# The second feed-forward unit as eight products, and fewer, wider operations on the hidden activations

## The reference, cut to what matters

```python
def swiglu(hn, w_gate, w_up, w_down):
    return (jax.nn.silu(hn @ w_gate) * (hn @ w_up)) @ w_down
```

## Time and profile before

| what | us |
|---|---|
| median of 3 runs | 965.77 (965.2 to 968.26) |
| the profiled execution's own time | 965.3 |
| its span, first to last instruction | 963.2 |
| PE busy | 903.3 (94%) |
| VectorE busy | 662.5 (69%) |
| ScalarE busy | 452.3 (47%) |
| GpSimd busy | 234.3 (24%) |
| feed-forward units, first to last matmul | 582.5 to 949.5 |

### The profile page before, as it was taken

The page is one execution under the profiler, slowest core; times in us unless marked ns, Lnnn a source line. Parts: engine busy times, 40 slices in busy tenths (PEclk is TensorE's granted clock), DMA queues, the critical chain, the costliest instruction groups (busy, mean ns, idle before and its releaser), DMA issues.

```text
span 963.2 us, 17847 instructions
## 1 busy us (share of the span) xinstructions
PE 903.3 (94%) x7198; PEld 829.3 (86%) x7198; DVE 662.5 (69%) x1272; ACT 452.3 (47%) x831; POOL 234.3 (24%) x163
## 2 busy tenths in 40 slices
PE   5999999889999999999989998899999998999997
PEld 4999998756799889975569898899999998999996
DVE  4799974565445796121553678998869999779765
ACT  5553125566454473135425545455445555345442
POOL 3000001103000033300020022444544444545540
PEclk9999999899999999999999989799999999999999
DMA  8222206422442359268052003222242222222232
GB/s 231 91 86 89 89 2 230 161 71 88 138 131 76 103 182 329 100 233 335 9 168 66 24 1 137 88 89 88 90 127 91 88 88 89 88 88 88 99 126 93
DMA packets 81554, 110.55 MB, mean 115 GB/s; under 512 B 9505, under 2 KB 64674, under 8 KB 81090
## 3 DMA queue, kind: packets, MB, share of 16 engines
q1 hardware_dynamic: 81248, 109.37, 34.0%
q10 hardware_dynamic: 226, 0.05, 0.0%
HBM read 100.48 MB, written 8.93 MB: 114 GB/s over the span
## 4 chain that ended last, share of the span: by engine, by line
PE 70%; DVE 19%; issue 5%; ACT 4%; DMA 1%; SPq 1%; DVEq 0%; POOL 0%; ACTq 0%
PE pall L2303 20%; PE pall L2879 17%; PE pall L2315 6%; PE pall L2657 5%; PE pall L2888 4%; PE pall L2340 4%; DVE ring_lo L1412 2%; DVE pall L1409 2%; DVE g_part L1412 2%; PE pall L2708 2%; PE pall L2373 1%; DVE g_part_f L1406 1%; PE pall L2727 1%; PE pall L2327 1%; PE pall L2533 1%
## 5 line engine op out<-in xcount | busy, mean ns | idle before, releaser
L817 POOL TENSOR_TENSOR ring_lo<-w_raw,ring_hi 128x512 fp32r<-128x512 f32 (+1 forms) x128 | 174.2, 1374 | 266.0 <-ACT ring_hi L1271 265.2
L2879 PE MATMUL pall<-x_hi,ring_hi 128*128 128x272 f32 x304 | 91.2, 300 | 13.8 <-DVE gate_odd L1409 5.7
L2879 PE MATMUL pall<-x_sum,ring_hi 128*128 128x272 f32 x456 | 89.1, 291 | 4.3 <-ACT sq L1299 4.3
L2879 PE MATMUL pall<-x_lo,ring_hi 128*128 128x272 f32 x304 | 90.2, 297 | 0.0
L2879 PE MATMUL pall<-x_hi,ring_lo 128*128 128x272 f32 x304 | 90.1, 296 | 0.0
L1271 ACT ACTIVATE ring_hi<-w_raw 128x512 fp32r<-128x512 f32 (+1 forms) x128 | 75.4, 612 | 26.5 <-PE pall L2879 17.2
L2879 PE MATMUL pall<-g_part,ring_hi 128*128 128x272 f32 x448 | 84.5, 288 | 1.9 <-DVE z_down L1409 1.9
L2879 PEld LDWEIGHTS pall<-x_sum,ring_hi 128*128 128x128 f32 x456 | 73.0, 191 | 4.5 <-ACT sq L1299 4.5
L2303 PE MATMUL pall<-x_hi,w_hi 128*128 128x272 f32 x352 | 73.6, 290 | 0.5 <-issue 0.5
L2879 PEld LDWEIGHTS pall<-x_hi,ring_hi 128*128 128x128 f32 x304 | 59.8, 197 | 15.5 <-DVE gate_odd L1409 6.4
L2303 PE MATMUL pall<-x_hi,w_lo 128*128 128x272 f32 x352 | 72.9, 288 | 0.0
(11 more groups left out here) (464 smaller groups left out, 2393.8 us busy)
## 6 DMA issues: line engine op xcount, KB each, us to landing
w_raw<-in_w_gate SPq DMA_DIRECT2D x10, 1024.0 KB, 5.3
w_raw<-in_w_up SPq DMA_DIRECT2D x10, 1024.0 KB, 5.3
w_raw<-in_w_in SPq DMA_DIRECT2D x8, 1024.0 KB, 5.7
w_raw<-in_w_down SPq DMA_DIRECT2D x8, 1024.0 KB, 5.0
dm_kv<-in_cache_mem_v SPq DMA_DIRECT2D x5, 1024.0 KB, 14.2
w_raw<-in_w_out SPq DMA_DIRECT2D x4, 1024.0 KB, 9.0
d_k<-in_cache_k SPq DMA_DIRECT2D x16, 256.0 KB, 2.9
d_v<-in_cache_v SPq DMA_DIRECT2D x16, 256.0 KB, 3.9
```

Source lines behind the costliest of these rows:

```text
L817: e.tensor_tensor(w_part(ring_lo[:, q % RING, :], n), sev_source(n, i), w_part(ring_hi[:, q % RING, :], n).bitcast(F32), ALU.subtract)\
L2879: ins = mm(out, w, x, start=i in SEV_FIRST and j == 0 and s_, stop=j == np_ - 1 and t_, skip_group_check=i not in SEV_FIRST)
```

## The change

The diff does this: (1) n = 1 becomes classic, with eight products on banks 2, 3, 6, 7 (`first_unit`, `first_evac`); its weight sums, their low parts and its bank additions are gone. The unit that needs the input sums first is now n = 2, its weight sums lie in SBUF, and the last input sum waits for 14 instead of 7 products' count. (2) For pairs 0 to 7 the seven blocks are rounded by one ScalarE instruction of 1904 columns and one VectorE subtraction of 1904 columns; both wait for the last difference. (3) The differences b12-b11 and b12-b22 are one instruction of 544 columns with b12 repeated; places 2 to 4 change their order, and small memsets that only signalled are gone. (4) In gate units, the scalings of banks B and C by `rstd` are one instruction; the even units' banks are renumbered so that B and C are neighbours. (5) The low part for product 2 moves behind the first bank addition, and the low parts of the activations move behind both halves of the weight sums.

```diff
     def classic(n):
-        return n == 0 or n >= DOWN_2
+        return n < 2 or n >= DOWN_2
...
+    def first_banks(n):
+
+        return [bank(i)[:, 0:HALF] for i in ((4, 5, 0, 1), (2, 3, 6, 7))[n]]
...
     def sev_banks(n):
-        return [bank(i)[:, 0:HALF] for i in ((2, 3, 4) if n % 2 else (0, 1, 5))]
+        return [bank(i)[:, 0:HALF] for i in ((2, 3, 4) if n % 2 else (5, 0, 1))]
     def sums_in_banks(n):
-        return 2 <= n < DOWN_2
+        return 3 <= n < DOWN_2
...
-    G_PLACE, G_BATCH = (0, 2, 3, 6, 4, 1, 5), (1, 2, 2, 3, 2, 1, 3)
+    G_PLACE = (0, 2, 4, 6, 3, 1, 5)
     def g_cut(p, i):
-        return (slice(0, 2), slice(2, 3) if plain(p) else slice(2, 5), slice(6, 7) if plain(p) else slice(5, 7))[i]
+        return (slice(0, 2), slice(2, 3), slice(6, 7))[i] if plain(p) else slice(0, 7)
+
+    def batches(p):
+
+        return range(3 if plain(p) else 1)
+
+    def g_batch(p, i):
+
+        return sum(len(batches(x)) for x in range(p)) + i + 1
...
             if t == 3:
-                e.wait_ge(S("sev_p"), 7)
+                e.wait_ge(S("sev_p"), 14)
...
-            e.wait_ge(S("g_made"), 3 * p + i + 1)
+            e.wait_ge(S("g_made"), 3 * p + (i + 1 if plain(p) else 3))
...
-        sev_hi(1, 0)
-        sev_hi(1, 1)
-        for i in range(3):
-            g_hi(0, i)
+        for i in pieces(1):
+            sev_hi(1, i)
         silu(1, 0)
-        for i in range(2, 7):
-            sev_hi(1, i)
+        g_hi(0, 0)
+        sev_hi(2, 0)
+        silu(1, 1)
+        for i in range(1, 7):
+            sev_hi(2, i)
         x_sum_hi(3)
...
             elif before == "up":
-                g_hi(p, 1)
+                g_hi(p, 1 if plain(p) else 0)
             sev_copy(n, 1)
             sev_copy(n, 2)
-            if before == "up":
+            if before == "up" and plain(p):
                 g_hi(p, 2)
             for i in range(1, 6):
                 sev_hi(n + 1, i)
-            if what == "up":
+            if what == "up" and plain(at_):
...
-                if n > 1:
+                if n > 2:
                     e.wait_ge(*low_ready(n - 1, 1))
-                if n == 2:
-                    e.wait_ge(acc_out, J_FFN + 8)
+                if n == 3:
+                    e.wait_ge(S("sev_out"), 8)
...
         def g_sums(p, b12):
-            b11, b22, t1, t2, t3, t4, b21 = (g_part_f[:, p % GROUP, 7 + i, :] for i in range(7))
-            sub(t3, b12, b22)
-            done(sub(t1, b12, b11))
-            done(sub(t2, b22, t1))
+            f = g_part_f[:, p % GROUP, 7:14, :]
+            done(sub(f[:, 2:4, :], b12.rearrange("p (o t) -> p o t", o=1).broadcast_to([P, 2, HALF]), f[:, 0:2, :]))
+            sub(f[:, 4, :], f[:, 1, :], f[:, 2, :]).then_inc(S("g_made"), 1)
         def g_last(p):
-            b21, t4, t2 = (g_part_f[:, p % GROUP, 7 + i, :] for i in (6, 5, 3))
-            sub(t4, b21, t2).then_inc(S("g_made"), 1)
+            f = g_part_f[:, p % GROUP, 7:14, :]
+            e.wait_ge(S("g_made"), 3 * p + 2)
+            sub(f[:, 5, :], f[:, 6, :], f[:, 4, :]).then_inc(S("g_made"), 1)
         def g_low(p, i):
             at_ = g_cut(p, i)
-            if i == 1:
-                e.wait_ge(S("g_made"), 3 * p + 3)
-            e.wait_ge(S("g_hi"), 3 * p + i + 1)
+            e.wait_ge(S("g_made"), 3 * p + 3)
+            e.wait_ge(S("g_hi"), g_batch(p, i))
...
-                return
             in_bank = what != "down"
             ended(3)
             add(B_ if in_bank else u0[:, H0], u0[:, H0], B_).then_inc(out, 1)
+            sum_low(n + 1, 2)
             ended(4)
             add(u1[:, H1], u1[:, H1], A_).then_inc(out, 1)
...
             elif what == "gate":
-                e.wait_ge(out, 4 * n + 1)
-                mul(u0[:, H0], B_, rstd[:, H0])
                 e.wait_ge(out, 4 * n + 2)
                 mul(u1[:, H1], u1[:, H1], rstd[:, H1])
             sum_low(n + 1, 5)
...
             if what == "gate":
                 e.wait_ge(out, 4 * n + 3)
-                mul(u0[:, H1], C_, rstd[:, H1]).then_inc(S("gate_r"), 1)
+                both = pall[:, 3:5, 0:HALF] if n % 2 else pall[:, 0:2, 0:HALF]
+                mul(u0.rearrange("p (a t) -> p a t", a=2), both, rstd[:].rearrange("p (a t) -> p a t", a=2)).then_inc(S("gate_r"), 1)
                 ended(6)
                 mul(u1[:, H0], A_, rstd[:, H0]).then_inc(out, 1)
...
                     done(mul(C_, C_, g0[:, H1]))
                     g_sums(p, C_)
-                    e.memset(small[:, 61:62], 0.0).then_inc(S("g_made"), 1)
...
+        def first_evac(n, m):
+
+            e.wait_ge(S("sev_p"), 7 * n + 4 + 3 * m)
+            b = first_banks(n)[2 * m:2 * m + 2]
+            f = g_part_f[:, 1, 7:14, :]
+            if n == 0:
+                for a, h in enumerate((H0, H1)):
+                    mul(gate_tile(1, m)[:, h], b[a], rstd[:, h]).then_inc(S("sev_out"), 1)
+                if m == 0:
+                    e.wait_ge(S("sev_out"), 2)
+                    e.memset(small[:, 61:62], 0.0).then_inc(S("gate_r"), 1)
+            else:
+                e.wait_ge(S("silu"), 4)
+                places = (f[:, 6, :], f[:, 1, :]) if m else (f[:, 0, :], sq[:, 0, H1])
+                for a, h in enumerate((H0, H1)):
+                    mul(places[a], b[a], gate_tile(1, m)[:, h]).then_inc(S("sev_out"), 1)
...
-        weight_sums(1, (1, 2))
-        sev_evac(0)
-        sum_low(1, 5)
+        first_evac(0, 0)
+        first_pair()
+        first_evac(0, 1)
+        weight_sums(2, (1, 2))
+        g_low(0, 0)
+        sum_low(2, 1)
+        first_evac(1, 0)
+        sum_low(2, 2)
+        first_evac(1, 1)
+        e.wait_ge(S("sev_out"), 8)
+        e.memset(small[:, 61:62], 0.0).then_inc(S("g_made"), 1)
+        sum_low(2, 5)
+        g_sums(1, sq[:, 0, H1])
+        g_last(1)
+        input_low(3)
...
             before, p = sev[n - 1][:2]
             adds = what == "down" and at_[0] > 0
-            if before == "up":
-                g_low(p, 0)
             weight_sums(n + 1, (1,))
-            if n == 1:
-                input_low(3)
-                for i in range(3):
-                    g_low(0, i)
-            if before == "up":
-                g_low(p, 1)
             if adds:
                 sev_add(n, 0)
             weight_sums(n + 1, (2,))
             if adds:
                 sev_add(n, 1)
+            if before == "up":
+                for i in batches(p):
+                    g_low(p, i)
             sum_low(n + 1, 1)
             if adds:
                 sev_add(n, 2)
-            if before == "up":
-                g_low(p, 2)
-            sum_low(n + 1, 2)
             sev_evac(n)
...
-                if at_[1] == 0:
-                    e.wait_ge(S("g_lo"), 3 * p + G_BATCH[i])
+                if at_[1] == 0 and i == 0:
+                    e.wait_ge(S("g_lo"), g_batch(p, 0))
...
-                    e.wait_ge(*((S("sev_out"), 4 * (n - 1)) if n >= 2 else (acc_out, J_FFN + 6)))
-                elif i == 1 and n == 1:
-                    e.wait_ge(S("sev_out"), 2)
+                    e.wait_ge(S("sev_out"), 4 * (n - 1))
...
-        def first_gate():
+        def first_unit(n):
             for m in range(2):
-                e.wait_ge(acc_out, J_FFN + (2 if m else 4))
+                e.wait_ge(acc_out, J_FFN + ((4, 2), (6, 8))[n][m])
                 for k in range(2):
...
-        first_gate()
-        for n in range(1, DOWN_2):
+        first_unit(0)
+        first_unit(1)
+        for n in range(2, DOWN_2):
             seven(n)
```

More of the change, by code:

```diff
@@ L1346, in _ @@
         x_sum_hi(2)
-        sev_hi(1, 0)
-        sev_hi(1, 1)
-        for i in range(3):
-            g_hi(0, i)
+        for i in pieces(1):
+            sev_hi(1, i)
         silu(1, 0)
-        for i in range(2, 7):
-            sev_hi(1, i)
+        g_hi(0, 0)
[3 more added lines that the diff above has]
+            sev_hi(2, i)
         x_sum_hi(3)
         for n, (what, at_, np_) in enumerate(sev):
-            if n == 0:
+            if n < 2:
                 continue
@@ L1373, in _ @@
             if before == "gate":
-                if p > 1:
-                    silu(p, 0)
+                silu(p, 0)
                 silu(p, 1)
             elif before == "up":
-                g_hi(p, 1)
+                g_hi(p, 1 if plain(p) else 0)
             sev_copy(n, 1)
             sev_copy(n, 2)
-            if before == "up":
+            if before == "up" and plain(p):
                 g_hi(p, 2)
@@ L2119, in sev_evac @@
                     e.wait_ge(S("sev_p"), 7 * group_end(p // GROUP - 1))
[L2120 to L2123, removed]
-                        ins = mul(gate_tile(1, m)[:, h], bank((4, 5, 0, 1)[2 * m + a])[:, 0:HALF], rstd[:, h]).then_inc(out, 1)
-                    if m == 0:
-                        e.wait_ge(out, 2)
-                        e.memset(small[:, 61:62], 0.0).then_inc(S("gate_r"), 1)
-                        sum_low(1, 1)
-                        first_pair()
```

(20 more changed lines are left out.)

1 line of the change is left out of this document (removed).

## The result

The changed kernel takes 953.5 us (median of 4 runs, 951.9 to 955.1), the kernel before 967.0 (965.2 to 971.2): ratio 0.986, 95% interval 0.983 to 0.989. Timed again later with six runs it took 953.95, ratio 0.987 (0.984 to 0.990). That is 13.5 us less; forecast were 9.5 less, 956.3, and a range of 949.8 to 962.

A forecast was written before the change was run, and what follows sets the result against it. VectorE's work up to each gate unit's second bank addition was taken as the bound. Savings of 7.65 + 1.3 + 0.55 = 9.5 us turned the profiled 965.3 into 955.8, median 956.3 us; range 949.8 to 962.

The forecast's parts named there:

- The bound and the second unit: VectorE bounds gate and up units; PE runs unit 1 without a stop, and unit 2's mark comes 7.0 us earlier.
- the mark: The time at which VectorE reaches the second bank addition of a gate unit; forecast 7.0 us earlier in unit 2.
- the 2 us of cover: During unit 1, VectorE would finish the sums of unit 2 and then wait about 2 us for the unit's end.
- Unit 4 and 6: Marks of the next two gate units after unit 2, near 643 and 666 us; 7.65 us gained by unit 6.
- The charge of 1.05 for the lower clock: Added ahead of unit 4's mark, since the 3.0 us PE gap in unit 2 can bring the lower clock.
- The pair: Each pair of gate and up units saves 0.35 us of VectorE time, bounds -1.1 and 2.2.
- Low parts on VectorE: Activations' low parts in each pair: one instruction of 2.14 us for three in 2.27, saving 0.13.
- Moving the low parts: Low parts moved within gate units stand ahead of the mark before and after, so no work crosses it; no cost counted.
- Scaling: 0.07: Gate units: two scalings of 272 columns become one of 544, saving 0.07 us a pair.
- The second stretch: Units 11 to 18: four gate marks save 1.3 us, and a spared slow-clock window adds 0.55, 1.1 at even chance.
- The slower one: GpSimd, held up by the wide subtraction, causes two more meetings a pair, 1.8 us each pair; about 971.5 us, chance 0.06.
- The larger gain: The 1904-column subtraction starts before GpSimd's burst, removing two meetings in about three of six bound pairs; 950.5 us, chance 0.17.

The follow-up runs named there:

- part1b: Kernel before with only the second unit made classic, the activations' three low parts in their old places between the weight sums; stage 359.4 us against 366.85.
- late5_low2: Changed kernel with the third low part moved behind the unit's evacuation and product 2's low part behind the mark in gate units; 948.5 us, ratio 0.982.

## Why the prediction was right, and where it was not

**The bound and the second unit: right.** VectorE's way to the mark set the gate units. PE went through unit 1 without a stop; the mark of unit 2 was forecast 36.3 us after the first matmul and product 6 started at 36.30; PE's wait there, forecast 3.0, was 2.15, since PE reached it 0.85 late, 0.6 of it spent waiting for a copy. Worth 7.0 as forecast; alone, 7.5 over the whole stage. The load landed when forecast (its first sum starts 13.8 us into the stage). VectorE was there 0.8 early, then met GpSimd three times instead of at most once, and of the 2 us of cover 1.2 were left:

```profile
DVE w_sum L1421 <- DMA w_raw<-in_w_gate: 0.8, 1, 0.8
```

**Unit 4 and 6: 8.4 gained for 7.65.** Forecast were 60.45 and 83.55 after the start; measured 60.01 and 82.90. The charge of 1.05 for the lower clock was nearly right in this trace (23.7 for 22.9); in the second trace the same gap of 2.15 was followed by no lower clock, and the stage was 0.85 shorter. What follows a gap of this length isn't fixed, so this hit of the charge was luck.

**The pair: 0.35 forecast, 0.55 measured, and for other reasons.** This is the step that failed. "Low parts on VectorE: one of 2.14 for 2.27, saves 0.13" compared the instructions, and "Moving the low parts moves no work across the mark" took their place for free. At full clock the place alone costs 0.31 a pair and the one piece wins 0.87, because of what each does beside GpSimd's burst; over the stage, with the lower clock that followed the gaps, that is 6.1 and 11.7 in these traces. "Scaling: 0.07" saved is 0.58 lost. "Differences: 0.15" is 0.2. I had counted instructions and taken the meetings as given, and the sum came near only because errors of both signs met in it: that is luck. I had also taken the pair as one chain of VectorE. Of the 0.55, 0.23 were won ahead of the up unit's addition, and there the changed kernel has reached PE's pace; only what stands between that addition and the mark (13.03 of 22.9) can be shortened further.

**The second stretch: 1.85 forecast, 3.4 measured** between the marks of units 6 and 18 (11.81 less 8.39), from 0.67 up to unit 12, 0.55 and 0.57 in the next two pairs, and 1.6 in the pair that had run at the lower clock (24.5, now 22.9), which I had charged at even chance. After it 0.5 more came, most of it at down unit 19, whose wait fell from 1.3 to 0.8 us. Together 12.3 for 9.5.

**Rivals.** The slower one is out: the wide subtraction did hold GpSimd up, by 0.6 a burst, but it took 2.13 and the distance is 22.9, not above 24.5. The Trainium skill (SBUF — State Buffer, "Who interferes with whom") says of VectorE's two-port modes that whoever issues first gets the shared pair for the whole instruction. The pairs of rows above agree with it in both directions, for instructions with two SBUF inputs: GpSimd 0.14 us ahead, VectorE's 0.69 became 1.70; VectorE 0.14 ahead, GpSimd's 1.30 became 1.70. The larger gain had the right mechanism, the wide instruction ahead of the burst, but against the old place (`part1b`, 13.47 in the second part) it won little; its 950.5 and its distance of 22 aren't reached by the changed kernel.

**Open.** What decides whether the lower clock follows a gap. Of the twelve gaps of 2.06 to 2.18 us in these traces with a pair of units behind them, three were followed by a window at 0.93, two of them in the kernel before, where a third of the same 2.06 (at 762.18) was not; of eight gaps of 2.36 to 2.49, five were; of the longer ones 2.88 and 4.25 (twice) were and 3.30 was not. Not run was `late5_low2` with separate scalings. Its trace speaks against a further gain: the subtraction in the weights already takes 0.69 there, and VectorE waits 1.18 for ScalarE behind it.

## What to carry to other kernels

Where two engines exclude each other at a port, the cost of an instruction is its place: trace who was first in each pair of them, and put instructions that read PSUM, or a single long one that starts early, where the other engine has its burst. Undo each part of a merged change alone: of five parts here one cost 3 to 4 us that the others hid. Cut the repeated distance where the engine last waited for another: what is saved ahead of that point is waited away. Move work behind a wait only when the engine has idle time; while it is full the wait just changes its name.

## What the runs showed of the hardware

VectorE with two SBUF inputs beside GpSimd's subtraction: 0.69 us became 1.66 to 1.80 for 512 columns, and 2.13 became 3.23 for 1904; the other way round, GpSimd's 1.30 became 1.70. Instructions of 272 columns with one input in PSUM kept their 0.43 us inside GpSimd's burst. The time ahead of the stage, with the same code, spread over 12 us between traces, with the granted clock of the whole run between 0.976 and 0.996.
